# Neighbour attention: probabilities divided in place by GpSimd and turned by plain transposes, in place of products with a scaled diagonal

## Chip, cores, metric

The kernel runs on 1 core of one Trainium2 chip. The metric is the device time of one execution in microseconds, the median of several runs.

## What is computed

Two transformer-like blocks follow each other, on 1024 tokens of width 1024 (and 256 context tokens in the first block). The change touches one part of the first block, which has two layers: the neighbourhood attention. Its 1024 tokens are a grid of 16 rows and 64 columns. Each query attends to 8 grid rows and 16 columns around it, with a bias by relative place, and to all 256 context tokens, under one softmax:

```python
s_nb = jnp.einsum("bqhd,bmqnhd->bhqmn", q_r, k_nb).astype(jnp.float32)
...
s_nb = s_nb + jnp.transpose(bias, (0, 2, 1, 3)).astype(jnp.float32)[None]
s_ctx = jnp.einsum("bqhd,bchd->bhqc", q_r, k_ctx).astype(jnp.float32)
s = jnp.concatenate([s_nb.reshape(bsz, NA_HEADS, GRID_W, n_nb), s_ctx], axis=-1)
p = jax.nn.softmax(s, axis=-1).astype(v.dtype)
...
return (jnp.einsum("bhqmn,bmqnhd->bqhd", p_nb, v_nb)
        + jnp.einsum("bhqc,bchd->bqhd", p_ctx, v_ctx))
```

There are 4 heads of 64. In the first layer the 256 context tokens are queries too, and attend to the context alone.

## The kernel before

All of it is float32. The first block of each layer runs as stages with a barrier of all engines between them (`end_section`): projections, `attention_operands`, the dense attention (`pair_attention`), `neighbour_attention` (L1317), and the output product. `mixers` (L2163) calls the last but one with a list of *units*. A unit is 128 queries of a pair of heads. The keys that the grid rows of its queries can see are 4 or 5 tiles of 128, and the context is 2 more: 6 or 7 tiles, so 768 or 896 columns of scores; masked places get a large negative bias. The units of context queries have 2 tiles, 256 columns. The first layer has 20 units: 6, 6, 7, 7, 7, 7, 6, 6, 2, 2 tiles, twice. The second has 16, without the units of 2.

For each unit and head (`hh`) the work goes round the engines. TensorE makes the scores in PSUM (L1381). VectorE takes the maximum of the context's columns (L1438), adds the bias and takes the maximum of the rest in one custom instruction (L1440), and turns its sign (L1441). ScalarE takes the exponential and its sum (`exponential`, L1474), into `probs` in SBUF. VectorE takes the reciprocal of the sum (`invert`, L1427). GpSimd multiplies the 128x128 identity with that reciprocal, one for each partition, into `diag` (L1510). TensorE multiplies each 128x128 tile of `probs` with `diag` (`turn`, L1392): the product is the tile transposed and divided by the sum, in one. Up to four tiles go into one PSUM bank, a *group*; a unit with more than 4 tiles has four groups, in the order first half of head 0, first half of head 1, rest of head 0, rest of head 1. Groups use three banks in turn (`banks[t % 3]`), and a group waits until the one three before it has been copied (`wait_copied`). VectorE copies the first halves to `probs_t` (L1448), ScalarE the rest (L1482). TensorE multiplies the values with `probs_t` (`values`, L1403), and ScalarE copies the result out (L1489).

The order on each engine is written out by hand. TensorE runs, for each i, scores(i), values(i-2), turn(i-1). Scores(i) wait until both exponentials of unit i-1 are done, since they overwrite the same PSUM. VectorE runs the reciprocals of unit i-1, the maxima of unit i, and then its copies of unit i-1. ScalarE runs exponential of head 0, the output copy of i-2, exponential of head 1, and its copies of unit i-1. `probs`, `diag` and `probs_t` have two buffers each, by i % 2.

GpSimd has a second task in the loop: the pooling branch (`Pooling`, L1681), whose plan of 20 steps (15 in the second layer) `advance` spreads over all units but the last three, behind each unit's two diagonals: clearing buffers, copies, shifted sums (L1736), means (L1744) and differences (L1746). Some units get one step and some two, and a step has up to two instructions. Behind two of the last units it makes the lower halves of the next stage's first weights (`ahead.low`, L241). After the loop TensorE applies the pooling weights (`pooling.mix`, L1756).

Of the kernel before, what the change touches and what calls it, by code (L numbers as in the profile page):

```python
# [15 lines left out]
ALU = mybir.AluOpType  # L16
# [5 lines left out]
P = 128  # L22
# [140 lines left out]
def keep_busy(pg, bank, times):  # L163

    for _ in range(times):
        pg.nc.tensor.matmul(bank[:, 0:P], pg.dense[:], pg.dense[:], start=True, stop=True)
# [1150 lines left out]
def neighbour_attention(pg, cn, units, v_of, pooling_in, ahead):  # L1317
# [14 lines left out]
    nc = pg.nc  # L1332
    n = len(units)
    rows = (slice(0, HD), slice(HD, P))
    groups, by_dve, by_act, before = [], [], [], [0]
# [7 lines left out]
    width = [sum(cw for c0, cw, k0 in u[2]) for u in units]  # L1343
    with ExitStack() as st:
        probs = pg.sbuf(st, "probs", [P, 2, 2, BANK + P + CTX])
        probs_t = pg.sbuf(st, "probs_t", [P, 2, 2, 7, P])
        diag = pg.sbuf(st, "inverse_diagonal", [P, 2, 2, P])
        ctx_max, neg_max, sums, inv_sums = (pg.sbuf(st, k, [P, 2, 2]) for k in ("ctx_max", "neg_max", "sums", "inv_sums"))
        banks = [pg.aux[:, 0, :]] + [pg.acc[:, b, 2 * BANK:] for b in range(2)]
        value = pg.aux[:, 1, 0:P]  # L1350
        scored, max_ready, exp_done = pg.sem("scored"), pg.sem("max_ready"), pg.sem("exp_done")
        inverted, diag_ready, turned = pg.sem("inverted"), pg.sem("diagonal_ready"), pg.sem("turned")
        dve_copied, act_copied = pg.sem("copied_by_dve"), pg.sem("copied_by_act")
        out_ready, out_copied, own = pg.sem("out_ready"), pg.sem("out_copied"), pg.sem("dve_step")
        pooling = pooling_in(st)
# [4 lines left out]
        def wait_copied(eng, count):  # L1360
            eng.wait_ge(dve_copied, sum(g < count for g in by_dve))
            if any(g < count for g in by_act):
                eng.wait_ge(act_copied, sum(g < count for g in by_act))

        with nc.Block() as block:
            @block.sync
            def _(sp):
                pooling.sync(sp)
                ahead.fetch(sp)

            @block.tensor
            def _(pe):
                def scores(i):
                    q, k, pieces, bias, tiles = units[i]
                    if i == 1:
                        keep_busy(pg, banks[0], 8)
                    if i >= 1:
                        pe.wait_ge(exp_done, 2 * i)
                    for c0, cw, k0 in pieces:
                        for hh in range(2):  # L1380
                            mm = nc.tensor.matmul(pg.acc[:, hh, c0:c0 + cw], q[rows[hh]], k[rows[hh], k0:k0 + cw], start=True, stop=True)  # L1381
                            if c0 + cw == width[i]:
                                mm.then_inc(scored, 1)

                def turn(i):
                    for t in range(before[i], before[i + 1]):
                        _, hh, first, m = groups[t]
                        pe.wait_ge(diag_ready, 2 * i + hh + 1)
                        if t >= 3:
                            wait_copied(pe, t - 2)  # L1390
                        for j in range(m):
                            mm = nc.tensor.matmul(banks[t % 3][:, j * P:(j + 1) * P], probs[:, i % 2, hh, (first + j) * P:(first + j + 1) * P],  # L1392
                                                  diag[:, i % 2, hh], start=True, stop=True)
                        mm.then_inc(turned, 1)

                def values(i):
                    tiles = units[i][4]
                    wait_copied(pe, before[i + 1])
                    if i >= 1:
                        pe.wait_ge(out_copied, i)  # L1400
                    for j, t in enumerate(tiles):
                        for hh in range(2):
                            mm = nc.tensor.matmul(value[rows[hh]], v_of(i, t, hh), probs_t[:, i % 2, hh, j], start=(j == 0), stop=(j == len(tiles) - 1))  # L1403
                    mm.then_inc(out_ready, 1)

                for i in range(n + 2):
                    if i < n:
                        scores(i)
                    if i >= 2:
                        values(i - 2)  # L1410
                    if 1 <= i <= n:
                        turn(i - 1)
                    if i == n:
                        for m in range(n_mixed):
                            t = len(groups) + m
                            wait_copied(pe, t - 2)
                            pooling.mix(pe, m, banks[t % 3]).then_inc(turned, 1)

            @block.vector
            def _(dve):  # L1420
                step = Counter(dve, own)

                def invert(i, hh):
                    dve.wait_ge(exp_done, 2 * i + hh + 1)
                    if i >= 2:
                        dve.wait_ge(diag_ready, 2 * (i - 2) + hh + 1)
                    nc.vector.reciprocal(inv_sums[:, i % 2, hh:hh + 1], sums[:, i % 2, hh:hh + 1]).then_inc(inverted, 1)  # L1427

                def maximum(i, hh):
                    q, k, pieces, bias, tiles = units[i]  # L1430
                    dve.wait_ge(scored, 2 * i + hh + 1)
                    m = neg_max[:, i % 2, hh:hh + 1]
                    local = width[i] - CTX
                    if local == 0:
                        nc.vector.tensor_reduce(m, pg.acc[:, hh, 0:CTX], AX_X, ALU.max, negate=True).then_inc(max_ready, 1)
                        return
                    first = ctx_max[:, i % 2, hh:hh + 1]
                    step.done(nc.vector.tensor_reduce(first, pg.acc[:, hh, local:width[i]], AX_X, ALU.max))  # L1438
                    s = pg.acc[:, hh, 0:local]
                    step.done(nc.vector.tensor_tensor_reduce(s, s, bias[hh], 1.0, first, ALU.add, ALU.max, m))  # L1440
                    nc.vector.tensor_scalar(m, m, -1.0, None, ALU.mult).then_inc(max_ready, 1)  # L1441

                def copy(t):
                    i, hh, first, m = groups[t]
                    dve.wait_ge(turned, t + 1)
                    if i >= 2:
                        dve.wait_ge(out_ready, i - 1)
                    nc.vector.tensor_copy(probs_t[:, i % 2, hh, first:first + m], banks[t % 3][:, 0:m * P].rearrange("p (a n) -> p a n", n=P)).then_inc(dve_copied, 1)  # L1448

                for i in range(n + 1):  # L1450
                    for hh in range(2):
                        if i >= 1:
                            invert(i - 1, hh)
                    for hh in range(2):
                        if i < n:
                            maximum(i, hh)
                    if i >= 1:
                        for t in range(before[i - 1], before[i]):
                            if t in by_dve:
                                copy(t)  # L1460
                for m in range(n_mixed):
                    t = len(groups) + m
                    dve.wait_ge(turned, t + 1)
                    pooling.keep(dve, m, banks[t % 3]).then_inc(dve_copied, 1)
                dve.wait_ge(dve_copied, len(by_dve))
# [35 lines left out]
            @block.gpsimd  # L1501
            def _(pool):
                pooling.begin(pool)
                steps, spread = len(pooling.plan), n - 3
                for i in range(n):
                    for hh in range(2):
                        pool.wait_ge(inverted, 2 * i + hh + 1)
                        if i >= 2:
                            pool.wait_ge(turned, before[i - 1])
                        nc.gpsimd.tensor_scalar(diag[:, i % 2, hh], cn["ident"][:], inv_sums[:, i % 2, hh:hh + 1], None, ALU.mult).then_inc(diag_ready, 1)  # L1510
                    if i < spread:
                        pool.wait_ge(diag_ready, 2 * i + 2)
                        pooling.advance(pool, i * steps // spread, (i + 1) * steps // spread)
                    elif i < spread + 2:
                        ahead.low(pool, i - spread)
                pool.wait_ge(ahead.parted, 2)
# [2583 lines left out]
```

## Time and profile before

| | us |
|---|---|
| median of 3 runs | 3808.54 (3807.89 to 3814.36) |
| the profiled execution, as timed | 3815.39 |
| its span in the profile | 3813.6 |
| TensorE busy | 3580.8 (94%) |
| VectorE busy | 2053.8 (54%) |
| GpSimd busy | 1875.9 (49%) |
| ScalarE busy | 1208.8 (32%) |

A float32 matmul (L1381, L1392, L1403) leaves two records in the trace; the records' count stands behind the shape (x28 are 14 products). Ends of matmuls are modelled, so the spacing of their starts says more than the length of one. A timeline row merges like instructions: start, length of the merged run, engine, line, what it writes and reads. "[2.27 <-ACT probs]" is idle time of the engine ahead of it, and whom it waited for.

### The profile page before, as it was taken

To read this page: it belongs to the slowest core of one execution; us is meant where nothing else is said; L and a number is where in the kernel's file an instruction comes from. 1 tells how busy PE (TensorE), PEld (TensorE's weight loads), DVE (VectorE), ACT (ScalarE), POOL (GpSimd) and SP (SyncE) were. 2 spreads that over 40 slices of the span, in tenths; PEclk is the share of its full clock that TensorE was granted. 3 is DMA by queue.
4 is the path that set the end of the run, shared out by engine and by line. 5 is a ranking of instruction groups with operands and counts; after the bars stand their busy time and mean duration, and the time that the engine had idled before them with its cause. 6 is when DMAs were issued, how large, how long until landed. Compare 5 with 4: busy or idle time off the path is not lost. (4 is left out here: it accounts for less than half of the span.)

```text
span 3813.6 us, 54938 instructions
## 1 busy us (share of the span) xinstructions
PE 3580.8 (94%) x22742; PEld 2769.6 (73%) x22742; DVE 2053.8 (54%) x2358; ACT 1208.8 (32%) x1716; POOL 1875.9 (49%) x1064
## 2 busy tenths in 40 slices
PE   5999899889899999889999999998899899999998
PEld 5888644578788754578887777876577688878877
DVE  4443577553444467563466733546542788784242
ACT  3224344431223354432123421324400444441020
POOL 1443266544254266543355643303633799974433
PEclk9999899999999999999999999999999899999999
DMA  4112200025211200022221220020043122234212
GB/s 186 39 39 68 70 1 1 27 87 199 80 35 60 61 1 1 26 100 89 82 74 50 75 94 26 4 100 1 1 143 112 61 94 83 83 110 163 60 49 72
DMA packets 101935, 258.02 MB, mean 68 GB/s; under 512 B 29232, under 2 KB 38576, under 8 KB 100800
## 3 DMA queue, kind: packets, MB, share of 16 engines
q1 hardware_dynamic: 83008, 215.42, 16.5%
q10 hardware_dynamic: 18688, 39.20, 3.1%
q8 instruction: 176, 2.88, 0.3%
q14 instruction: 63, 0.52, 0.0%
HBM read 200.02 MB, written 54.56 MB: 67 GB/s over the span
## 5 line engine op out<-in xcount | busy, mean ns | idle before, releaser
L1848 PE MATMUL acc<-h_hi,weights_hi 128*128 128x512 f32 (+1 forms) x928 | 347.0, 374 | 9.8 <-DVE h_lo L2017 7.4
L1850 PE MATMUL acc<-h_hi,weights_lo 128*128 128x512 f32 (+1 forms) x928 | 338.7, 365 | 0.0
L1849 PE MATMUL acc<-h_lo,weights_hi 128*128 128x512 f32 (+1 forms) x928 | 338.5, 365 | 0.0
L1093 DVE TENSOR_REDUCE part_max<-aux 128x1 f32<-128x428 f32 (+5 forms) x468 | 252.8, 581 | 151.3 <-PE aux L934 108.4
L2555 PE MATMUL acc<-h_hi,weights_hi 128*128 128x512 f32 x672 | 271.1, 403 | 0.0
L2557 PE MATMUL acc<-h_hi,weights_lo 128*128 128x512 f32 x672 | 263.0, 391 | 0.0
L2556 PE MATMUL acc<-h_lo,weights_hi 128*128 128x512 f32 x672 | 262.4, 390 | 0.0
L2031 DVE RECIPROCAL arena<-arena 128x512 f32<-128x512 f32 (+1 forms) x48 | 141.7, 2953 | 223.3 <-ACT arena L1994 223.3
L1055 ACT ACTIVATE probs<-acc 128x1024 f32<-128x1024 f32 (+1 forms) x168 | 168.4, 1003 | 239.3 <-PE acc L969 236.5
L980 PE MATMUL acc<-probs,v_tok 128*64 128x512 f32 (+3 forms) x864 | 218.2, 585 | 2.5 <-DVE inverse L1113 2.4
L3723 PE MATMUL acc<-operand_hi,weights_hi 128*128 128x512 f32 x504 | 197.6, 392 | 11.6 <-POOL weights_lo L3457 11.6
L1848 PEld LDWEIGHTS acc<-h_hi,weights_hi 128*128 128x128 f32 x928 | 175.4, 189 | 44.8 <-issue 11.7
L1849 PEld LDWEIGHTS acc<-h_lo,weights_hi 128*128 128x128 f32 x928 | 175.4, 189 | 32.8 <-issue 4.8
L3725 PE MATMUL acc<-operand_hi,weights_lo 128*128 128x512 f32 x504 | 197.3, 391 | 0.0
L3724 PE MATMUL acc<-operand_lo,weights_hi 128*128 128x512 f32 x504 | 197.1, 391 | 0.0
L1850 PEld LDWEIGHTS acc<-h_hi,weights_lo 128*128 128x128 f32 x928 | 175.3, 189 | 28.3
L968 PE MATMUL acc<-q_both_parts,k_twice 128*128 128x512 f32 (+3 forms) x432 | 179.0, 415 | 1.4 <-ACT q_and_shift L1027 1.2
L2618 POOL TENSOR_TENSOR weights_hi<-weights,ones 128x1024 fp32r<-128x1024 f32 x40 | 78.2, 1954 | 200.1 <-PE acc L2557 174.3
L1164 POOL TENSOR_TENSOR total<-total,probs 128x1024 f32<-128x1024 f32 (+1 forms) x72 | 159.2, 2211 | 26.3 <-ACT probs L1055 10.4
L934 PE MATMUL aux<-k_twice,q_both_parts 128*128 128x428 f32 (+7 forms) x468 | 151.6, 402 | 20.5 <-DVE part_max L1093 9.8
L969 PE MATMUL acc<-q_and_shift,k_rest_and_one 65*128 65x512 f32 (+3 forms) x432 | 164.6, 382 | 0.0
L1893 POOL TENSOR_TENSOR square_parts<-square,square_parts 128x512 fp32r<-128x512 f32 (+1 forms) x48 | 55.3, 1152 | 220.8 <-ACT square_parts L1988 220.8
(525 smaller groups left out, 9125.9 us busy)
## 6 DMA issues: line engine op xcount, KB each, us to landing
weights<-in_w_in SPq DMA_DIRECT2D x44, 512.0 KB, 3.5
arena<-in_w_mod SPq DMA_DIRECT2D x6, 2048.0 KB, 8.7
weights<-in_w_up SPq DMA_DIRECT2D x24, 512.0 KB, 4.2
weights<-in_w_out SPq DMA_DIRECT2D x22, 512.0 KB, 4.4
weight_sums<-feed_forward_spill SPq DMA_DIRECT2D x22, 512.0 KB, 4.4
xT<-in_w_up SPq DMA_DIRECT2D x20, 512.0 KB, 4.2
weights<-in_w_mod SPq DMA_DIRECT2D x4, 2048.0 KB, 26.2
mixer_gates<-arena SPq DMA_DIRECT2D x32, 256.0 KB, 2.0
```

What stands on the lines that cost most here:

```text
L968: nc.tensor.matmul(tile[:, hh], twice[:, at], qs[:, p % 2, hh, cols], start=True, stop=False)
L980: mm = nc.tensor.matmul(outs[blk % 2][halves[hh], skip:qn], pairs[p].v(t, hh), probs[:, e % ring, hh, skip:qn], start=i == 0, stop=e == bl ...
L1093: nc.vector.tensor_reduce(part_max[:, b % 2, j, hh, i:i + 1], max_tile(m)[:, hh, 0:cw], AX_X, ALU.max, negate=True).then_inc(max_done, 1)
L1848: nc.tensor.matmul(out, w_hi[:, b, k, :], hi[:, k, cols], start=(k == 0), stop=False)
L1849: nc.tensor.matmul(out, w_hi[:, b, k, :], lo[:, k, cols], start=False, stop=False)
L1850: return nc.tensor.matmul(out, w_lo[:, b, k, :], hi[:, k, cols], start=False, stop=(k == KD - 1))
L2555: nc.tensor.matmul(out, high[:, b, k, :], hi[:, k, at], start=(k == 0), stop=False)
L2556: nc.tensor.matmul(out, high[:, b, k, :], lo[:, k, at], start=False, stop=False)
L2557: return nc.tensor.matmul(out, low[:, b, k, :], hi[:, k, at], start=False, stop=(k == KD - 1))
L3723: nc.tensor.matmul(out, w.hi[:, o, j, :], operands[0][:, o, j, :], start=start, stop=False)
L3724: nc.tensor.matmul(out, w.hi[:, o, j, :], operands[1][:, o, j, :], start=False, stop=False)
L3725: return nc.tensor.matmul(out, w.lo[:, o, j, :], operands[0][:, o, j, :], start=False, stop=stop)
```

## The change

GpSimd no longer makes a diagonal. It multiplies the unit's whole row of probabilities (all 896, 768 or 256 columns of a head) by the reciprocal, in place. TensorE turns the divided tiles with the transpose instruction and the plain identity. The buffer `diag` goes; the semaphore `diag_ready` becomes `divided`, with the same counts. GpSimd's wait for `turned`, which kept `diag` from being overwritten, goes with it.

```diff
--- before.py
+++ after.py
@@ -1344,12 +1344,11 @@
     with ExitStack() as st:
         probs = pg.sbuf(st, "probs", [P, 2, 2, BANK + P + CTX])
         probs_t = pg.sbuf(st, "probs_t", [P, 2, 2, 7, P])
-        diag = pg.sbuf(st, "inverse_diagonal", [P, 2, 2, P])
         ctx_max, neg_max, sums, inv_sums = (pg.sbuf(st, k, [P, 2, 2]) for k in ("ctx_max", "neg_max", "sums", "inv_sums"))
         banks = [pg.aux[:, 0, :]] + [pg.acc[:, b, 2 * BANK:] for b in range(2)]
         value = pg.aux[:, 1, 0:P]
         scored, max_ready, exp_done = pg.sem("scored"), pg.sem("max_ready"), pg.sem("exp_done")
-        inverted, diag_ready, turned = pg.sem("inverted"), pg.sem("diagonal_ready"), pg.sem("turned")
+        inverted, divided, turned = pg.sem("inverted"), pg.sem("divided"), pg.sem("turned")
         dve_copied, act_copied = pg.sem("copied_by_dve"), pg.sem("copied_by_act")
         out_ready, out_copied, own = pg.sem("out_ready"), pg.sem("out_copied"), pg.sem("dve_step")
         pooling = pooling_in(st)
@@ -1385,12 +1384,12 @@
                 def turn(i):
                     for t in range(before[i], before[i + 1]):
                         _, hh, first, m = groups[t]
-                        pe.wait_ge(diag_ready, 2 * i + hh + 1)
+                        pe.wait_ge(divided, 2 * i + hh + 1)
                         if t >= 3:
                             wait_copied(pe, t - 2)
                         for j in range(m):
-                            mm = nc.tensor.matmul(banks[t % 3][:, j * P:(j + 1) * P], probs[:, i % 2, hh, (first + j) * P:(first + j + 1) * P],
-                                                  diag[:, i % 2, hh], start=True, stop=True)
+                            mm = nc.tensor.transpose(banks[t % 3][:, j * P:(j + 1) * P], probs[:, i % 2, hh, (first + j) * P:(first + j + 1) * P],
+                                                     cn["ident"][:])
                         mm.then_inc(turned, 1)
 
                 def values(i):
@@ -1423,7 +1422,7 @@
                 def invert(i, hh):
                     dve.wait_ge(exp_done, 2 * i + hh + 1)
                     if i >= 2:
-                        dve.wait_ge(diag_ready, 2 * (i - 2) + hh + 1)
+                        dve.wait_ge(divided, 2 * (i - 2) + hh + 1)
                     nc.vector.reciprocal(inv_sums[:, i % 2, hh:hh + 1], sums[:, i % 2, hh:hh + 1]).then_inc(inverted, 1)
 
                 def maximum(i, hh):
@@ -1505,11 +1504,10 @@
                 for i in range(n):
                     for hh in range(2):
                         pool.wait_ge(inverted, 2 * i + hh + 1)
-                        if i >= 2:
-                            pool.wait_ge(turned, before[i - 1])
-                        nc.gpsimd.tensor_scalar(diag[:, i % 2, hh], cn["ident"][:], inv_sums[:, i % 2, hh:hh + 1], None, ALU.mult).then_inc(diag_ready, 1)
+                        prob = probs[:, i % 2, hh, 0:width[i]]
+                        nc.gpsimd.tensor_scalar(prob, prob, inv_sums[:, i % 2, hh:hh + 1], None, ALU.mult).then_inc(divided, 1)
                     if i < spread:
-                        pool.wait_ge(diag_ready, 2 * i + 2)
+                        pool.wait_ge(divided, 2 * i + 2)
                         pooling.advance(pool, i * steps // spread, (i + 1) * steps // spread)
                     elif i < spread + 2:
                         ahead.low(pool, i - spread)
```

## Rows read from the trace of the kernel before

**Rows 1.** The page, first line and section 1: busy time of each engine.
```profile
span 3813.6 us, 54938 instructions
...
PE 3580.8 (94%) x22742; PEld 2769.6 (73%) x22742; DVE 2053.8 (54%) x2358; ACT 1208.8 (32%) x1716; POOL 1875.9 (49%) x1064
```

**Rows 2.** Windows view, both loops; columns in its first line.
```profile
core 0: us, PE busy (x) PEld busy (x) DVE busy (x) ACT busy (x) POOL busy (x), PEclk, DMA share, GB/s
...
708.00:841.00 133.00, 125.42 (x1140) 100.55 (x1140) 78.56 (x222) 56.23 (x134) 65.53 (x65) 0.97 0.09 29
1572.00:1690.00 118.00, 112.33 (x1050) 91.21 (x1051) 70.85 (x197) 51.08 (x114) 53.02 (x51) 0.98 0.09 30
```

**Rows 3.** Timeline of the first loop, one iteration with 7 tiles.
```profile
740.92 1.78 PE L1381 MATMUL acc<-arena 64*128 64x512 f32 x12
...
742.63 1.75 PE L1403 MATMUL aux<-probs_t,arena 128*64 128x128 f32 x28
...
744.31 2.05 PE L1392 MATMUL acc<-inverse_diagonal,probs 128*128 128x128 f32 x16
...
745.76 1.33 DVE L1448 COPY probs_t<-acc 128x512 f32<-128x512 f32 x2
...
746.78 0.19 ACT L1474 ACTIVATION_READ_ACCUMULATOR probs<-acc,neg_max 128x1 f32 x1
...
747.01 0.21 DVE L1427 RECIPROCAL inv_sums<-sums 128x1 f32<-128x1 f32 x2
...
747.32 1.18 POOL L1510 TENSOR_SCALAR inverse_diagonal<-ident,inv_sums 128x128 f32<-128x128 f32 x2 [2.90 <-PE aux L1392]
747.63 0.70 PE L1381 MATMUL acc<-arena 64*128 64x512 f32 x2
```

**Rows 4.** Timeline of the first loop, around an early TensorE.
```profile
768.32 1.56 PE L1381 MATMUL acc<-arena 64*128 64x512 f32 x8
...
773.59 0.19 ACT L1474 ACTIVATION_READ_ACCUMULATOR probs<-acc,neg_max 128x1 f32 x1
...
773.83 2.33 PE L1381 MATMUL acc<-arena 64*128 64x512 f32 x8 [2.27 <-ACT probs L1474]
...
780.37 1.13 PE L1381 MATMUL acc<-arena 64*128 64x512 f32 x4
```

**Rows 5.** Waits of TensorE and of GpSimd in the first loop: total us, times, longest.
```profile
PE acc L1381 <- ACT probs L1474: 3.5, 2, 2.3
...
POOL inverse_diagonal L1510 <- PE acc L1392: 19.1, 8, 5.2
POOL inverse_diagonal L1510 <- PE aux L1392: 18.5, 6, 5.2
```

**Rows 6.** Lines L1510, L1392, L1234: ns min/median/max, starts; timeline of transposes.
```profile
L1510 POOL TENSOR_SCALAR inverse_diagonal<-ident,inv_sums x72: 600/602/607, 714.7 to 1675.3; 128x128 f32<-128x128 f32 x72
...
L1392 PE MATMUL acc<-inverse_diagonal,probs x578: 275/275/377, 718.1 to 1678.9; 128*128 128x128 f32 x193
...
L1234 PE MATMUL aux<-ident,arena x60: 272/273/447, 389.3 to 1312.3; 128*128 128x128 f32 x60
...
406.47 1.04 PE L1234 MATMUL aux<-ident,arena 128*128 128x128 f32 x8
```

**Rows 7.** GpSimd by form in the first loop; busy us, mean ns of one, idle before.
```profile
L1510 POOL TENSOR_SCALAR inverse_diagonal<-ident,inv_sums 128x128 f32<-128x128 f32 x40 | 23.7, 602 | 53.3 <-PE acc L1392 19.1 <-PE aux L1392 18.5 <-DVE inv_sums L1427 9.2
...
L1744 POOL TENSOR_TENSOR padded<-padded,inv_count 128x1024 f32<-128x1024 f32 x2 | 4.7, 2358 | 0.2
...
L1728 POOL COPY padded<-arena 128x1024 f32<-128x1024 f32 x2 | 2.1, 1037 | 0.1
...
L1744 POOL TENSOR_TENSOR padded<-padded,inv_count 128x256 f32<-128x256 f32 x2 | 1.5, 727 | 0.2
...
L1728 POOL COPY padded<-arena 128x256 f32<-128x256 f32 x2 | 0.8, 397 | 0.1
```

**Rows 8.** Timeline of GpSimd, the longest pooling step.
```profile
748.59 2.33 POOL L1736 TENSOR_TENSOR padded<-padded 64x1288 f32<-64x1288 f32 x1
750.98 1.25 POOL L1738 COPY padded<-padded 64x1288 f32<-64x1288 f32 x1
752.31 2.36 POOL L1744 TENSOR_TENSOR padded<-padded,inv_count 128x1024 f32<-128x1024 f32 x1
```

**Rows 9.** Windows view, two stretches; columns as in rows 2.
```profile
40.00:60.00 20.00, 15.61 (x299) 13.49 (x299) 10.55 (x15) 5.70 (x11) 8.48 (x4) 1.00 0.21 78
...
768.00:780.00 12.00, 9.73 (x66) 6.72 (x65) 8.26 (x26) 4.31 (x11) 3.80 (x6) 0.86 0.00 0
```

## The prediction

> **What bounds the kernel now.** Times come from one profiled execution: a span of 3813.6 us [rows 1], 3815.4 us as timed; its median over three runs is 3808.5 us, so the forecast is made as a difference and set on 3808.5. The change touches one loop, run once in each layer of the first block: 133 us and 118 us of the span, with TensorE busy 94 to 95% of them and GpSimd half [rows 2]. Nothing outside it is changed, and the stages are divided by barriers, so only these 251 us can move.
>
> I call an iteration the stretch from one unit's scores to the next unit's. On TensorE it holds, in this order, the scores of unit i, the values of unit i-2, and the turning of unit i-1. The timeline of the one that starts at 740.92 shows two things that end almost together [rows 3]. TensorE: 1.71 us of scores, 1.68 of values, then 28 records of turning (two to a tile, 7 tiles, 2 heads) in 3.32 us, 0.119 each; sum 6.71, and the next scores start at 747.63, 6.71 later. The other is a round through VectorE and ScalarE: scores, two maxima, the second exponential, which ends 746.97, 6.05 after the start. Where TensorE is done early the next scores follow the exponential by 0.05 [rows 4], so this round alone would take 6.11. For units of 6 tiles it is 5.46+0.05=5.51 (768.32 to 773.83, where TensorE really did wait for ScalarE, 2.27 us [rows 4]); for the units of 2 tiles some 3.0. So TensorE bounds the iterations, with little behind it, and the round is late next. TensorE hardly waits in the whole first loop; GpSimd mostly waits for TensorE [rows 5].
>
> **TensorE, the products that become transposes.** A tile costs 2x0.119=0.237 us now. The kernel has plain float32 transposes of the same shape elsewhere, one record each (60 for 60 tiles) [rows 6]; eight of them take 1.04 us, the last of which is 0.273 by itself, so (1.04-0.273)/7=0.110 apiece at full clock [rows 6]. There are 224 tile-turnings in the first loop and 208 in the second: 432x0.127=55 us of TensorE time. Most of that is no gain: an iteration with 7 tiles falls from 6.71 to 1.71+1.68+14x0.110=4.93 on TensorE, but the round holds it at 6.11. A second floor lies just below: the fourth group of a unit uses the bank of the first, which VectorE copies only after its two maxima (0.68 us from 745.76 [rows 3], then 3 transposes: 5.9). I went unit by unit through both loops with these durations (20 units: 6,6,7,7,7,7,6,6,2,2 tiles, twice; 16 in the second layer), each iteration the later of the round, TensorE's sum and the bank. The kernel before comes out within 1.2 us of the trace over 115 us, the difference being one clock drop [rows 4]. With transposes and a divide that is never late, the loops shorten by 10.0 and 8.1 us. **18 us is the ceiling** of this change.
>
> **GpSimd, the divide.** Now it scales a 128x128 diagonal for each unit and head: 602 ns, 72 times, all alike [rows 6, 7]. Afterwards it goes over 896, 768 or 256 columns. The trace shows TENSOR_SCALAR at one size only, so the price per column is unknown, and the neighbours bound it [rows 7]. A COPY takes 397 ns for 256 columns and 1037 for 1024: 0.83 ns per column and 183 fixed. A TENSOR_TENSOR takes 727 and 2358: 2.12 per column, 183 fixed. All through 602 at 128 columns: with the slope of COPY 896 columns take 1.24 us; with that of TENSOR_TENSOR 2.23; if the fixed part is the same 183 and the whole rest is slope (3.3 ns per column), 3.14. I take the middle one: it is near the mean of the two ends, and an operation that costs 602 where COPY extrapolates to 289 and a two-input one to 454 is hardly as cheap per column as a COPY. So 2.23, 1.96 and 0.87 us for 7, 6 and 2 tiles.
>
> The Trainium skill speaks against my choice. Its GPSIMD Engine Reference (section 3.1) puts loops of at most two arithmetic operations at 1.03 cycles per element, and its section 4.1 calls one-input work roughly line-rate. By that page the estimate is about 0.86 ns per column, the case of the COPY slope below; the COPY row agrees with it, and no row here shows it for this operation.
>
> **Whether that is hidden.** The divide starts 0.3 us after an iteration begins (the reciprocals of both heads come behind VectorE's copies, at the iteration's edge [rows 3]). TensorE wants head 0 after scores and values, at 3.4, and head 1 at 3.9. At 2.23 head 1 is ready at 0.3+4.5+0.1=4.9, its ten transposes end at 6.0: just hidden in 6.11. What isn't hidden is the queue behind it. Between the divides GpSimd does the pooling steps and two splits of weights, in program order, and the next divide waits for them: 2.4 us in most iterations, and once 2.33+1.25+2.36, 6.1 with gaps [rows 8]. Take the iteration that starts at 747.63: divides until T+4.8, that step until T+10.9, divides of the next unit until T+14.8, its last eight transposes until T+15.7. Two iterations, 12.54 us before, take 15.7, and 16.8 with the delay that GpSimd brings along. In sum GpSimd has 115 us of work in the first loop (65.5 [rows 2] less 40x0.60, plus 16x2.23+16x1.96+8x0.87), against the 109 that the round would allow from its first unit on. Unit by unit with GpSimd's queue as a fourth bound, the first loop gives its 10.0 back and loses 12.4, the second gives its 8.1 back and loses 6.6: **+19 us**. The iterations that grow are those whose step holds two or three operations (9.9, 8.9 and 8.2 us in the first loop, 9.4 and 7.8 in the second).
>
> In those TensorE idles for some 2 to 4 us, six times. After its 2.27 us wait the next records ran at half speed and the iteration took 6.54 in place of 5.51; the granted clock of that stretch is 0.86 [rows 4, 9]. Half of that for six gaps, since part is hidden: +3. The wait for `turned` that GpSimd loses only held an engine that had nothing due; the freed diagonal and the renamed semaphore are on no path. The forecast is 3808.5+19+3 = **3830 us**.
>
> **The rivals.** (a) *Cheap columns*: slope 0.83 to 1.2. Same walk: -13 at 0.83, some -8 at 1.2; 3796 to 3801 us. For it: COPY. Against: 602 ns at 128 columns would need 495 fixed, against 183 of two other operations. (b) *Even*: slope 1.2 to 1.8, from -7 to +8, crossing zero at 1.55 (896 columns in 1.8 us); about 3810. (c) *All of it in the slope*: 3.3 ns, 3.14 us; two divides alone (6.3) then exceed the round and GpSimd bounds every iteration: +71 and +3, 3882. (d) *The clock*: if transposes and the gaps of about 1 us before the fourth group let the granted clock fall to the lower level (1.2 GHz), scores cost 1.7 more, on the round itself: 7.8 for 6.5 on average in 30 iterations, about +40, 3850, whatever the divide costs. Against it: 20 us at full clock with TensorE busy for 15.6 [rows 9], and transposes between products at full speed at 406.47 [rows 6]. The Trainium skill's TensorE: Matmul & The Clock Gate (Part 4) states that transpose mode doesn't count as activity for the clock; row 406.47 neither shows nor excludes it for 6 us stretches. (e) *The transposes are not shorter here* (they run as two records each): the divides come on top, about 3845.
>
> **How the numbers follow.** Forecast (slope 1.8 to 2.9; 3817 to 3852) 0.42; (a) 0.20; (b) 0.18; (c) 0.12; (d) 0.05; (e) 0.03. Within 0.2% (7.6 us, about what a measurement of this kernel can tell from no change): (b), 0.18. Faster: (a), 0.20. Slower: the rest, 0.62. As the cases of both signs are apart, the range is wide: from the end of (a), 3796, to (c), 3882, with more than a tenth of the chance close to or beyond its two ends.
>
> **What would show it.** The TENSOR_SCALAR of 896 columns: 1.2, 2.2 or 3.1 us; this decides nearly all. The transposes: 432 records at about 0.110. TensorE's waits: none but for ScalarE and VectorE if (a) holds, for GpSimd's divide if I am right, longest where the pooling step is long. The iteration at 740.92: 6.1. The granted clock of both loops: 0.97 and 0.98 before, some 0.93 if I am right, well below with (d). I am wrong above all if the slope of one operation is.

## The result, and the profile after

The changed kernel takes 3872.19 us (median of 4 runs, 3859.87 to 3875.28), the kernel before 3808.23 in runs beside it: ratio 1.0152, interval 1.0127 to 1.0178, some +58 us by the ratio. On a second chip, with more runs, it was 3852.8 against 3812.7, ratio 1.0105, interval 1.0086 to 1.0124, some +40 us. Slower, as forecast (3830, range 3796 to 3882), but by 2.6 and 1.8 times the 22 us that were worked out.

The page of the profiled execution, first line and section 1 (beside [rows 1]):

```profile
span 3873.5 us, 54036 instructions
...
PE 3583.8 (93%) x22310; PEld 2748.4 (71%) x22310; DVE 2051.9 (53%) x2358; ACT 1207.4 (31%) x1716; POOL 1992.1 (51%) x1064
```

The windows view of the two loops, to set beside [rows 2]; its columns are those of the first line:

```profile
core 0: us, PE busy (x) PEld busy (x) DVE busy (x) ACT busy (x) POOL busy (x), PEclk, DMA share, GB/s
707.00:856.00 149.00, 111.49 (x876) 76.32 (x876) 78.98 (x222) 55.20 (x134) 124.37 (x65) 0.87 0.05 17
1591.00:1721.00 130.00, 95.07 (x810) 65.62 (x811) 71.46 (x196) 50.02 (x114) 109.29 (x51) 0.93 0.06 20
```

TensorE is busy 75% and 73% of the loops in place of 94 to 95%, GpSimd 83% and 84% in place of 49% and 45%. From the first scores to the idle products that open the next stage, the first loop takes 149.2 us in place of 127.5, the second 129.6 in place of 113.2: +38.1. The span is 59.9 longer. So 22 us more were lost outside the code that was changed. That is a balance, as the experiments will show: unchanged stages ahead of 2500 us gave some 9 us back, one stage after it lost 22, and what follows it lost another 9.

GpSimd's divides by form in the first loop (busy us, mean ns, idle before), beside [rows 7], and the source view of the transposes, beside [rows 6]:

```profile
L1508 POOL TENSOR_SCALAR probs<-probs,inv_sums 128x896 f32<-128x896 f32 x16 | 40.2, 2523 | 3.0 <-DVE inv_sums L1426 2.5
L1508 POOL TENSOR_SCALAR probs<-probs,inv_sums 128x768 f32<-128x768 f32 x16 | 35.1, 2203 | 12.2 <-DVE inv_sums L1426 11.8 <-POOL arena L1744 0.2
L1508 POOL TENSOR_SCALAR probs<-probs,inv_sums 128x256 f32<-128x256 f32 x8 | 7.3, 922 | 1.1 <-DVE inv_sums L1426 1.0
```

```profile
L1391 PE MATMUL acc<-ident,probs x289: 272/273/476, 717.5 to 1711.7; 128*128 128x128 f32 x145
...
L1391 PE MATMUL aux<-ident,probs x143: 272/273/476, 715.5 to 1712.0; 128*128 128x128 f32 x143
```

Three sizes give a straight line: (2523-922)/640=2.50 ns per column and 282 ns fixed. At 128 columns that is 602, the price of the diagonal before, to the nanosecond. There are 432 transposes with one record each.

TensorE's waits in the first loop (us in total, times, longest), beside [rows 5], where it waited for no divide at all:

```profile
PE acc L1391 <- POOL probs L1508: 21.9, 16, 2.9
PE aux L1391 <- POOL probs L1508: 6.9, 5, 1.8
```

One iteration with 7 tiles in the timeline, the counterpart of [rows 3]:

```profile
740.32 1.78 PE L1380 MATMUL acc<-arena 64*128 64x512 f32 x12
...
740.70 5.02 POOL L1508 TENSOR_SCALAR probs<-probs,inv_sums 128x896 f32<-128x896 f32 x2 [1.22 <-DVE inv_sums L1426]
...
742.04 1.75 PE L1402 MATMUL aux<-probs_t,arena 128*64 128x128 f32 x28
...
743.72 0.66 PE L1391 MATMUL acc<-ident,probs 128*128 128x128 f32 x4
...
745.78 0.65 PE L1391 MATMUL acc<-ident,probs 128*128 128x128 f32 x4 [1.41 <-POOL probs L1508]
...
747.02 1.34 PE L1380 MATMUL acc<-arena 64*128 64x512 f32 x6
```

TensorE is through with scores and values 3.4 us after the start, and with the first half of head 0 at 4.05. The divided head 1 comes at 5.46 (0.38+5.02+0.06), and TensorE has stood idle for 1.41 us. The iteration takes 6.70: what the transposes saved is what the divide costs, and 6.71 before becomes 6.70. And then the queue behind it, GpSimd's timeline, beside [rows 8]:

```profile
748.26 5.02 POOL L1508 TENSOR_SCALAR probs<-probs,inv_sums 128x896 f32<-128x896 f32 x2
753.37 2.33 POOL L1734 TENSOR_TENSOR padded<-padded 64x1288 f32<-64x1288 f32 x1
755.76 1.25 POOL L1736 COPY padded<-padded 64x1288 f32<-64x1288 f32 x1
757.09 2.35 POOL L1742 TENSOR_TENSOR padded<-padded,inv_count 128x1024 f32<-128x1024 f32 x1
759.54 4.38 POOL L1508 TENSOR_SCALAR probs<-probs,inv_sums 128x768 f32<-128x768 f32 x2
```

GpSimd doesn't wait once in this stretch. From the end of one pair of divides to the end of the next it is 10.6 us, and two iterations here take 8.65 and 9.33 us where they took 6.50 and 6.04.

### The profile page after: what moved, and what is told of

Read it like the earlier page. It is cut to its first block and busy times, and to the rows that moved or that the text cites. A ratio compares the mean times of both kernels' runs of the same rounds, so it can differ in the third digit from the quotient of the medians.

```text
span 3873.5 us, 54036 instructions
## 1 busy us (share of the span) xinstructions
PE 3583.8 (93%) x22310; PEld 2748.4 (71%) x22310; DVE 2051.9 (53%) x2358; ACT 1207.4 (31%) x1716; POOL 1992.1 (51%) x1064
## 5 line engine op out<-in xcount | busy, mean ns | idle before, releaser
L1508 POOL TENSOR_SCALAR probs<-probs,inv_sums 128x768 f32<-128x768 f32 (+2 forms) x72 | 157.8, 2203 | 25.8 <-DVE inv_sums L1426 23.8
```

## The experiments

Theory A: the two loops lose by the divide on TensorE's path and, more, by the pooling steps queued with it on GpSimd. Rival B: they lose by transposes and gaps that let TensorE's clock fall. For the 22 us outside, theory C: an unchanged stage of the second block loses its clock depending on the moment at which it is reached. Rival D: the change does it, in some way of its own. To compare places in the trace I take the start of the same VectorE instruction in each profile: one each around the loops (707.0 and 841.1, 1571.0 and 1690.0 in the kernel before), and one that starts at 2500.7 in the kernel before, some 40 us ahead of the end of the recurrent scan of the second block; I call that start the arrival. *The stage* is what runs from there to a VectorE instruction that starts at 2560.4 in the kernel before. By these instructions the changed kernel's loops are 20.8 and 16.4 us longer, 37.2 together. All that lies outside the loops is unchanged; of the changed kernel's other 22.7 us, 22.5 lie in the stage, and the rest (-8.7 ahead of it, +8.9 behind it) cancels.

**One part of the change alone: the divide.**

```diff
-mm = nc.tensor.transpose(banks[t % 3][:, j * P:(j + 1) * P], probs[...], cn["ident"][:])
+mm = nc.tensor.matmul(banks[t % 3][:, j * P:(j + 1) * P], probs[...], cn["ident"][:], start=True, stop=True)
```

> GpSimd divides in place as in the changed kernel, but TensorE turns the tiles by float32 products with the plain identity. Theory A (the time in the two loops is lost to the divide, 282 ns + 2.50 ns per column, and to the pooling steps queued behind it; TensorE's shortening hides under that): the same walk through the units gives loops 23.6 and 17.0 us longer than before, so only 3 to 5 us worse than the changed kernel in both loops together. Rival B (the transposes and the clock that falls with them cost the time): without transposes the loops lose clearly less than the 38 us of the changed kernel. The part outside the loops (+22 us in the changed kernel) is not settled by this run; by theory C (it depends on the moment at which the stage at 2500 us is reached) it may come out as anything from 0 to 25.

Loops +26.0 and +17.2, together 43.2 (the walk through the units, as in the prediction: 40.6). The total is 3876.7 against 3817.5 on its chip. So the transposes are not to blame: even beside a divide this long they bring 6 us (37.2 for 43.2), and without them the kernel is no faster. TensorE waits for the divide here too. B is out as the main cause.

**The other part alone: the transposes.**

```diff
 # before's code, GpSimd's diagonals and all waits unchanged
-mm = nc.tensor.matmul(banks[t % 3][:, j * P:(j + 1) * P], probs[...], diag[:, i % 2, hh], start=True, stop=True)
+mm = nc.tensor.transpose(banks[t % 3][:, j * P:(j + 1) * P], probs[...], cn["ident"][:])
```

> Part of the computation left out: the probabilities are not divided by their sums. TensorE turns them by transposes, while GpSimd goes on making the scaled diagonals, so that all waits stay. Theory A: this shows the ceiling, loops 10.0 and 8.1 us shorter than before, the iteration with 7 tiles 6.1 us, 432 transposes at 0.110. Rival B (transposes let the clock fall): the granted clock in the loops falls from 0.97 and 0.98 below 0.9 and the loops are not shorter.

This leaves the division by the sum out. Loops -10.6 and -6.3, together -16.9 of the 18.1 that were the ceiling. The windows view of both loops:

```profile
709.00:826.00 117.00, 95.37 (x876) 67.09 (x876) 77.63 (x222) 54.00 (x134) 65.44 (x65) 0.98 0.07 22
1562.00:1669.00 107.00, 90.28 (x809) 64.03 (x810) 70.08 (x196) 48.68 (x114) 52.89 (x51) 0.95 0.07 24
```

In the first loop TensorE is busy only 82%, over a third of that with transposes, and the clock is at 0.98, beside 0.97 before. In the second it is at 0.95, beside 0.98, and the loop is shorter all the same. The total is 3801.3 against 3817.5, ratio 0.9947 (0.9922 to 0.9973), although the profiled execution lost 19.8 us in the stage at 2500 us.

**The divide moved to ScalarE.**

```diff
-nc.gpsimd.tensor_scalar(prob, prob, inv_sums[:, i % 2, hh:hh + 1], None, ALU.mult).then_inc(divided, 1)
...
 # scalar engine, behind its copies of unit i - 1
+if i < n:
+    for hh in range(2):
+        act.wait_ge(inverted, 2 * i + hh + 1)
+        prob = probs[:, i % 2, hh, 0:width[i]]
+        nc.scalar.activation(prob, prob, ACT.Copy, scale=inv_sums[:, i % 2, hh:hh + 1]).then_inc(divided, 1)
```

> The change with the divide on ScalarE, in place, behind its copies of the unit before; GpSimd is left with the pooling steps. ScalarE stands idle some 2.5 to 3 us before the first exponential of every iteration, and an activation over 896 columns takes 1.01 us there, so two fit. Theory A: loops 8 to 10 and 6 to 8 us shorter than before, all in all 3791 to 3797 us if the rest stays as it was. Rival B: no shorter than before, since transposes and gaps let the clock fall.

3800.9 against 3817.5, ratio 0.9952 (0.9927 to 0.9976): faster than the kernel before and the changed one. It is above the 3791 to 3797 that I expected; its profile lost 6.5 us in the stage at 2500 us. Loops -11.7 and -8.0, together 19.7, which is 1.6 more than the ceiling as worked out. An iteration from its timeline:

```profile
736.06 1.78 PE L1380 MATMUL acc<-arena 64*128 64x512 f32 x12
...
736.54 1.97 ACT L1499 ACTIVATE probs<-probs,inv_sums 128x896 f32<-128x896 f32 x2
737.77 1.75 PE L1402 MATMUL aux<-probs_t,arena 128*64 128x128 f32 x28
...
739.45 1.09 PE L1391 MATMUL acc<-ident,probs 128*128 128x128 f32 x8
739.51 1.01 ACT L1473 ACTIVATE probs<-acc,neg_max 128x896 f32<-128x896 f32 x1
...
742.16 1.56 PE L1380 MATMUL acc<-arena 64*128 64x512 f32 x8
```

The two divides (1.05 us each on average over this loop) overlap slightly and take 1.97 us here. They are done 2.45 us after the start, before TensorE asks at 3.4 and before the first exponential at 3.45. The iteration takes 6.10: the round through VectorE and ScalarE, as computed, now bounds it. Its 7-tile iterations are 6.10 or 6.11 but for one with a gap in the clock (6.46).

**The queue behind the divides.** The pooling steps that GpSimd does between the divides are left out.

```diff
-pool.wait_ge(divided, 2 * i + 2)
-pooling.advance(pool, i * steps // spread, (i + 1) * steps // spread)
+if i == spread - 1:
+    pool.wait_ge(divided, 2 * i + 2)
+    pool.sem_inc(pooling.pooled, 1)
```

> The changed kernel with the pooling branch's sums, means and differences left out (its matmul remains), so that GpSimd has only the divides in the loops, and the two splits of weights. Theory A (a third of the loss is the divide on TensorE's path, two thirds the pooling steps queued behind it): the walk gives 123.7 and 109.4 us for the two loops, 4.5 and 3.9 us longer than before, in place of 21 and 16; iterations of 7 tiles take 6.66. Rival B (the loss is the clock or the divide itself): the loops stay 12 us or more above before.

Loops +3.4 and +6.1, together 9.5 (the walk: 8.4), in place of 37.2. Three quarters of the loops' loss against the kernel before is the queue, one quarter the divide itself. Against the transposes alone (-16.9) the two weigh the same: 26 us for the divide, 28 for the queue. Most iterations with 7 tiles take 6.63 us. The total, of one run, is 3818.4 against 3812.7.

**The clock in the loops.**

```diff
-pe.wait_ge(divided, 2 * i + hh + 1)
 if t >= 3:
     wait_copied(pe, t - 2)
+if hh == 1 and first == 0 and m == 4:
+    keep_busy(pg, banks[t % 3], 5)
+pe.wait_ge(divided, 2 * i + hh + 1)
```

> The changed kernel with five idle products (1.1 us) on TensorE ahead of its wait for the divide of head 1, where it stood idle 1.4 to 1.5 us in each iteration. Theory A: the loops' loss is the divides and the queue behind them; less than 3 us of 38 go, since only some 26 us more at half clock lie in the first loop and much of that under waits. Rival B: it is the clock; time at half clock in the first loop falls from 36 us to below 12, and with it 8 to 12 us of the loss.

The windows view of its loops (the second window stops short of that loop's end):

```profile
706.00:855.00 149.00, 121.31 (x1025) 91.47 (x1026) 77.79 (x219) 54.83 (x133) 124.50 (x65) 0.90 0.05 17
1594.00:1712.00 118.00, 99.85 (x922) 77.64 (x923) 67.51 (x191) 49.08 (x111) 108.09 (x51) 0.97 0.07 22
```

The clock is somewhat higher (0.90 for 0.87, 0.97 for 0.93), the time isn't shorter: loops +24.0 and +14.0, together 38.0 for 37.2. The total is 3852.7 against 3812.7. By the windows shown, time at half clock in the first loop only fell from 39 to 29 us, not below 12 as B had it, so the test is weaker than planned; what it did raise brought nothing.

**Outside the loops.** First a pure delay, and both kernels again:

```diff
 # kernel before, end of TensorE's loop
+if n == 16:
+    keep_busy(pg, pg.acc[:, 0], 125)
```

> The kernel before with 125 idle products (28.4 us of TensorE) at the end of the loop of the second layer, so that all that follows comes 28.5 us later, as it does in the changed kernel when it reaches the stage at 2500 us. Theory C (the +22 us of the changed kernel from there on are the clock, and depend only on the moment at which that unchanged stage is reached): the same stretch of some 50 us at half clock appears, 28 + about 22 to 30 us in all, 3858 to 3868. Rival D (something else of the change, such as the placement of buffers, does it): +28.5 alone, 3837.

> The changed kernel once more, with many runs beside the kernel before on the same chip. In six profiles so far the unchanged stage at 2500 us took 5 to 22 us more than in the one profile of before, with 17 to 55 us more at half clock, in kernels with quite different times of arrival. Theory C2 (that stage's clock falls by chance in every kernel; the change is worth its two loops, +38 us, and the kernel before is as often hit when it is run often): the changed kernel comes out 35 to 45 us above before, ratio 1.009 to 1.012, and the loops again 20 to 22 and 16 to 17 us longer. Rival D2 (the change makes the fall in that stage more frequent): 50 to 65 us, 1.013 to 1.017.

> The kernel before, profiled once more. Theory C2: the stage at 2500 us has a stretch of 10 to 50 us at half clock here too, and takes 3 to 22 us more than in the first profile of the same kernel. Rival D2: it is as in the first profile, within 1 us.

The delay alone (loops -0.4 and +27.4) took 5.4 us more in the stage at 2500 us: the clock fell in a kernel that has nothing of the change, for 17 us and not for the 50 that were expected. Its total was expected at 3858 to 3868 and came out at 3846.6 against 3817.5, ratio 1.0088 (1.006 to 1.0116). That is 23 to 44 us, which doesn't tell the delay alone (28.5) from the delay with a short fall; the profile alone shows the fall. The changed kernel's second profile had +21.2 and +15.0 in the loops and +5.5 in that stage. Its ratio, 1.0105, is the one that theory C2 gave for the loops alone, and the 1.013 to 1.017 of rival D2 lie above its interval; the first measurement, 1.0152, lay within them. But the kernel before, profiled again, showed no fall, against C2, by which chance alone decides. What was left was the moment. Of the ten profiles so far, the three that arrive between 2499.7 and 2502.6 show no fall, and the seven others do. Two more, one delayed into that stretch and one out of it, were made to test that:

```diff
 # divide on ScalarE, as above, and at the end of TensorE's second loop
+if n == 16:
+    keep_busy(pg, pg.acc[:, 0], 108)
```

> The kernel with the divide on ScalarE, and 108 idle products (24.5 us) at the end of the second loop, so that it reaches the stage at 2500 us at the moment at which the kernel before does. So far three profiles that arrive at 2500 to 2503 us show no fall of the clock there, and seven that arrive elsewhere (2476 to 2543) show one, of 17 to 55 us. Theory C (the moment decides): no fall at half clock within 40 us of the mark, the stage within 3 us of before. Rival C2 (chance, or the kernel): a fall as in the same kernel without the delay, 5 us or more.

> The kernel before with 53 idle products (12 us) at the end of the second loop: arrival at about 2512 us, between the moments tried so far. Theory C: a fall, of 17 to 55 us, stage 5 to 22 us longer. Rival D (only a kernel whose neighbour attention is changed is hit): no fall, 12 us in all.

Both came as the moment has it, though not where they were aimed: the first arrived at 2504.9, 2 us behind the stretch known to be spared, and was spared; the second at 2509.0, and was hit. Each was run once (3818.9 and 3830.8 against 3814.9).

| profile | arrival | clock in some 60 us from there | stage, against before |
|---|---|---|---|
| kernel before, again | 2499.7 | 0.94 | -2.2 |
| kernel before | 2500.7 | 0.91 | 0 |
| pooling left out | 2502.6 | 0.94 | -2.1 |
| ScalarE divides, 24.5 us delay | 2504.9 | 0.94 | -2.0 |
| before, 12 us delay | 2509.0 | 0.82 | +6.8 |
| changed kernel, again | 2524.3 | 0.84 | +5.5 |
| before, 28.5 us delay | 2528.3 | 0.83 | +5.4 |
| changed kernel | 2529.2 | 0.54 | +22.5 |
| gap filled | 2534.1 | 0.84 | +5.5 |
| divide alone | 2542.5 | 0.74 | +13.0 |
| ScalarE divides | 2476.0 | 0.83 | +6.5 |
| transposes alone | 2479.5 | 0.54 | +19.8 |

The windows view of four of them, in the order before, changed, ScalarE with delay, before with 12 us delay:

```profile
2501.00:2561.00 60.00, 55.12 (x738) 46.72 (x732) 17.36 (x28) 13.03 (x24) 1.98 (x2) 0.91 0.39 157
```

```profile
2530.00:2590.00 60.00, 57.61 (x588) 49.02 (x586) 9.59 (x19) 7.52 (x17) 0.95 (x1) 0.54 0.09 32
```

```profile
2505.00:2565.00 60.00, 53.77 (x744) 45.29 (x740) 19.35 (x30) 13.23 (x24) 1.98 (x2) 0.94 0.39 157
```

```profile
2509.00:2569.00 60.00, 56.49 (x680) 47.52 (x680) 15.23 (x25) 13.06 (x23) 1.98 (x2) 0.82 0.25 102
```

In the changed kernel TensorE is busy for 57.6 of 60 us at hardly more than half speed, and gets through 588 records in place of 738. The fall comes 4.8 to 6.4 us after the arrival each time, behind the same wait for VectorE. TensorE's timeline of the changed kernel:

```profile
2533.14 0.69 PE L3105 MATMUL aux<-arena 128*64 128x64 f32 x16 [1.27 <-DVE arena L3195]
2533.75 0.68 PE L3108 MATMUL aux<-token_major,by_k 64*64 64x64 f32 x16
2534.26 0.71 PE L3115 MATMUL aux<-token_major 64*64 64x64 f32 x16
2534.90 1.97 PE L3121 MATMUL acc<-arena 128*128 128x64 f32 x8
```

The wait itself doesn't tell the hit profiles from the spared ones; the kernel before, which was spared, has it too:

```profile
2504.62 0.69 PE L3107 MATMUL aux<-arena 128*64 128x64 f32 x16 [1.27 <-DVE arena L3197]
```

How long a fall lasts goes with how soon it begins. Begun 4.8 or 4.9 us after the arrival (before with 12 us delay, ScalarE divides) it lasts 20.5 us; begun 5.2 or 5.5 after (transposes alone, changed kernel) 54.6 us; 6.1 after (divide alone) 30.7 us; 6.3 or 6.4 after (changed kernel again, gap filled, before with 28.5 us delay) 17.1 us. So the arrivals at 2528.3 and 2529.2 are near each other, but their falls begin almost a microsecond apart on that scale, and the one lasts three times as long as the other. What decides is then probably a timing finer than this table's, and it may be partly luck that the four spared arrivals lie within 5.2 us of each other. No run tests this.

The same happens ahead of all changed code. From 412.5 to 447.0 us, in an unchanged stage that all profiles reach within some 2 us of each other, the kernel before ran almost wholly at half clock and the changed kernel, profiled again, at full clock; by the end of that stage the second was 10 us ahead. The two in that order:

```profile
412.50:447.00 34.50, 31.46 (x168) 23.26 (x168) 18.11 (x30) 4.07 (x5) 0.00 (x0) 0.51 0.00 1
```

```profile
412.50:447.00 34.50, 29.16 (x253) 21.60 (x246) 25.55 (x46) 7.28 (x8) 1.51 (x5) 1.00 0.02 8
```

The next experiments fill that wait:

```diff
 if s == 0:
+    if n == 2 * (n_tiles - 2):
+        wait_used(pe, t, BY_K)
+        wait_used(pe, t, LAST)
+        keep_busy(pg, region[0], 4)
     pe.wait_ge(state_ready, n + 1)
```

> The divide on ScalarE, and four idle products (0.9 us) in the recurrent scan of the second block, ahead of TensorE's wait of 1.27 us behind which the clock fell (5 to 6 us after the mark, in each of the seven). If that wait is what lets the clock fall: no fall, the stage within 3 us of before, and 3785 to 3795 us in all, the fastest so far by some 8 us. If the small products of that stage let it fall: the fall stays and the time is that of the divide on ScalarE alone.

> The changed kernel itself with the same four idle products ahead of the wait in the recurrent scan. Theory A with C (the change costs 36 to 38 us in its two loops, and the rest of its first measurement, +22 us, was the clock's fall in the scan): no fall there, the stage within 3 us of before, loops 20 to 22 and 15 to 17 us longer, ratio to before 1.007 to 1.010 (before itself is hit in some of its runs). Rival D2 (the change has a cost of its own outside the loops): the stage stays 5 us or more above before.

With the divide on ScalarE and the wait filled: 3790.9 against 3814.9, ratio 0.9935 (0.9914 to 0.9956), the fastest kernel of all. It arrives at 2474.0, far from the spared moment, and its clock stays up. The changed kernel with the wait filled arrives at 2535.2, where its neighbours fell. TensorE's idle time in that wait is 0.18 and 0.19 us now, in place of 1.27. The windows view of both:

```profile
2474.00:2534.00 60.00, 54.98 (x752) 46.37 (x750) 19.43 (x29) 13.35 (x24) 1.98 (x2) 0.94 0.39 157
```

```profile
2535.00:2595.00 60.00, 56.22 (x722) 46.70 (x722) 15.77 (x26) 13.36 (x24) 1.98 (x2) 0.89 0.39 157
```

The second shows no fall 5 to 6 us after its arrival; its first stretch at half clock begins 36 us after it and lasts 3.4 us, and its 0.89 is a little below the 0.91 and 0.94 of the spared profiles. Its stage is 2.0 us longer than before's, its loops 23.6 and 16.6. The total is 3847.6 against 3822.7, ratio 1.0055 (1.0032 to 1.0078). Of the 1.007 to 1.010 that I expected only the lower end lies within that interval. The kernel before may be hit in some executions as well (its 13 runs there spread from 3808.7 to 3843.1), but no profile shows it in this stage, and the filled kernel's ten runs still spread by 17 us. Two filled profiles without a fall, where four of twelve unfilled ones had none, are evidence for the fill and not proof.

## Why the prediction was off

- *What bounds the kernel.* Right. The round of 6.11 and 5.51 us that lay below TensorE's 6.71 appeared as the iteration's length, to 0.01 us, when the divide went to ScalarE, and the ceiling of 18 us was measured as 16.9 and 19.7, a little to either side.
- *The transposes.* Right: one record, full speed between products, 55 us of TensorE time that is worth 18 at most.
- *The slope of the divide.* This step failed, as the text said that it would decide nearly all. I took 2.12 ns per column, the two-input slope; it is 2.50. So 896 columns take 2.52 us and not 2.23. The argument by which I chose, that an operation dearer at 128 columns than both neighbours is hardly cheaper per column, pointed the right way and stopped too soon: the operation is dearer per column than both. Its fixed part is 282 ns, between the neighbours' 183 and the 331 that my slope left. Rival (a), the COPY slope, is out by a factor of three. So is the estimate of 0.86 ns per column from the Trainium skill, GPSIMD Engine Reference, sections 3.1 and 4.1 (1.03 cycles per element, one-input work roughly at line-rate): this case's trace disagrees, and the measured 2.50 holds for this operation.
- *What the slope does.* The overlap failed with it: at 2.23 us head 1 was to be just hidden in an iteration of 6.1, at 2.52 TensorE waits 1.41 us for it and the iteration takes 6.70. With 2.50 and 282 in the same walk, the loops come out 20.5 and 14.6 us longer, 35.1 in all against 37.2 measured, iteration by iteration within 0.2 us in the plain ones with 7 tiles (6.66 against 6.57 to 6.70) and within a microsecond or so in the long ones (10.4 against 9.3, 10.1 against 11.0). A slope 18% higher doubled the loss, from 19 to 35 us, since GpSimd was near its limit. The term was mis-sized; the mechanism (the divide on TensorE's path, and the queue behind it) holds.
- *The clock in the loops.* I had +3 for six gaps and a clock of some 0.93. The clock was 0.87 in the first loop and 0.93 in the second, the measured loops exceed the walk by 2, and filling the gap changed nothing that can be told. Rival (d) is out: with transposes alone the clock stayed at 0.98 and 0.95 and the loops were 16.9 us shorter. The Trainium skill, TensorE: Matmul & The Clock Gate, Part 4, says that a transpose doesn't count as busy in the same way as other products; nothing in these loops shows a loss by it.
- *"Only these 251 us can move".* This step failed too, by 22 us in the first profile and 5 in the second, both in the stage at 2500 us. A barrier keeps work apart, not the clock. That unchanged stage, reached 28.5 us later, ran for 55 us at half clock. Its clock also falls in kernels that have nothing of the change (+5.4 and +6.8 us with a delay alone), and an unchanged stage ahead of the loops differs by up to 10 us between profiles. So these microseconds are no work of the change, and the size of the first measurement (+58, against +40 on the second chip) holds some luck.
- *Range and direction.* Slower was right, by the mechanism that was named. That 3872 lies within 3796 to 3882 says little: the range is wide, and of the loss only some 37 us come from the loops; the rest of the first measurement comes from a place that the prediction had ruled out.

What stays open: what in the moment decides whether the clock falls in that stage and for how long (17 or 55 us at arrivals of 2528.3 and 2529.2), and how often each kernel is hit in runs without a profile. That the moment decides rests on 12 profiles, two of them forecast; a chance of another kind that happens to fit them can't be excluded.

## What to carry to other kernels

Before moving an elementwise step from a small operand to a large one on GpSimd, measure that very operation at two sizes; one size and the neighbours' slopes left a factor of four. Count the engine's whole queue, not only the moved step: here three quarters of the net loss was other work, in program order behind the divides. The engine to ask first is the one that idles just when the input becomes ready; here ScalarE had 2 to 3 us free in the rounds with 6 or 7 tiles, and the same change became a gain. And before a difference of some 20 us is put down to a change, compare the same instruction's start in both profiles ahead of, within and behind the changed code, and profile each kernel twice.

## What was not expected of the hardware

GpSimd's TENSOR_SCALAR with a factor for each partition costs 282 ns and 2.50 ns per float32 column (602, 922, 2203 and 2523 ns at 128, 256, 768 and 896 columns), more per column than a TENSOR_TENSOR with two full inputs (2.12 [rows 7]). ScalarE does the same 896 columns in 1.05 us.

TensorE's clock can fall to its lower level (1.2 GHz) in a stretch of small products behind a wait of 1.27 us, and then stay there for 17 to 55 us, in the longest case with TensorE busy 96% of the time. In four of twelve profiles it did not fall in the same code behind the same wait. With four idle products in that wait, which leave 0.2 us of it, neither of the two kernels that were tried showed the fall.
